# A hybrid decoder step on one core: depthwise taps on VectorE alone, PEER queries block by block, V rows 20 steps behind U rows

## The reference

```python
xn = rmsnorm(h, g_mix);  z = xn @ w_in                       # 1024 -> 512 pool, 512 val, 512 gate
ya = pool_mixer(z[:, :512])                                  # trailing means over 2/4/8/16, minus token, @ w_pool, * scale
u  = z[:, 512:1024] * sigmoid(z[:, 1024:])
yb = silu(layernorm(causal_depthwise_conv(u, w_dw, 31 taps) + b_dw))
h  = h + concat(ya, yb) @ w_out
x  = rmsnorm(h, g_ffn)
q  = (x @ w_q)                                               # 8 heads, 2 halves of 128 channels
s  = q @ sub_keys^T                                          # 128 scores for each half
sv, si = top_k(s, 16)                                        # for each half
cand = sv[half 0][:, None] + sv[half 1][None, :]             # 256 candidates
top_s, top_j = top_k(cand, 16); eidx = (si0 * 128 + si1)[top_j]
gate = softmax(top_s)
coef = gate * gelu(x . u_tab[eidx])                          # a row of 1024 numbers for each (token, head, k)
h  = h + sum(coef * v_tab[eidx])                             # again a row of 1024 numbers each
h  = h + (p @ w_ple_proj) * sigmoid(rmsnorm(h, g_ple) @ w_ple_gate)
y  = rmsnorm(h, g_final)
```

## Time and profile before

| | |
|---|---|
| median of 3 runs | 3163.8 us |
| the profiled execution, its time | 3164.09 us |
| its span, first to last instruction | 3162.3 us |
| mean granted TensorE clock | 0.965 |
| busy: TensorE matmul / VectorE / ScalarE / GpSimd | 2740.3 / 2224.3 / 836.8 / 2096.6 us |
| DMA: moved, mean rate over the span | 1165.84 MB, 369 GB/s |
| of it by the indirect gathers (queue 0) | 1107.43 MB |

### The profile page before, as it was taken

The page is one execution under the profiler, slowest core; times in us unless marked ns, Lnnn a source line. Parts: engine busy times, 40 slices in busy tenths (PEclk is TensorE's granted clock), DMA queues, the critical chain, the costliest instruction groups (busy, mean ns, idle before and its releaser), DMA issues.

```text
span 3162.3 us, 25895 instructions
## 1 busy us (share of the span) xinstructions
PE 2740.3 (87%) x7017; PEld 1261.3 (40%) x7017; DVE 2224.3 (70%) x5506; ACT 836.8 (26%) x2010; POOL 2096.6 (66%) x2238
## 2 busy tenths in 40 slices
PE   8978999899789988888888877799988898779878
PEld 7754444344334434443444432244333343223322
DVE  8946787988876666777777766666667777666553
ACT  2232323232222222222222222332222322222212
POOL 2533657667776677666766767777777777776773
PEclk9989999999999999999999999999999999999999
DMA  5216999999999999999999999999999999999995
GB/s 149 70 38 232 401 386 391 400 374 395 409 409 401 397 408 404 405 403 402 395 403 395 406 407 398 405 398 397 408 409 409 406 408 397 409 409 396 408 409 201
DMA packets 388084, 1165.84 MB, mean 369 GB/s; under 512 B 35769, under 2 KB 113161, under 8 KB 387941
## 3 DMA queue, kind: packets, MB, share of 16 engines
q0 software_dynamic: 304128, 1107.43, 88.8%
q1 hardware_dynamic: 83280, 55.92, 5.9%
q10 hardware_dynamic: 533, 0.83, 0.1%
HBM read 1158.88 MB, written 5.15 MB: 368 GB/s over the span
## 4 chain that ended last, share of the span: by engine, by line
DMA 29%; PE 23%; DVE 19%; POOL 15%; issue 7%; ACT 1%; DVEq 0%; ACTq 0%; POOLq 0%
DMA ex_u_row<-in_u_tab_dram,ex_eidx 22%; PE ex_acc L1547 14%; POOL ex_v_row L1007 8%; DVE ex_u_row L1654 7%; POOL ex_u_row L1007 7%; DMA ex_v_row<-in_v_tab_dram,ex_eidx 6%; PE ex_q L1286 4%; DMA ex_u_row<-in_u_tab_dram,ex_few_idx 1%; PE ex_q L1337 1%; DVE ex_same L1593 1%; DVE ex_same L1597 1%; DVE ex_idx L1600 1%; PE ex_s L1419 1%; DVE ex_top_at L1573 1%; DVE ex_top_at L1566 1%
## 5 line engine op out<-in xcount | busy, mean ns | idle before, releaser
L1547 PE MATMUL ex_acc<-ex_v_row,ex_diag 128*128 128x512 f32 (+1 forms) x4176 | 1982.6, 618 | 365.6 <-DMA ex_v_row<-in_v_tab_dram,ex_eidx 196.6
L1654 DVE CUSTOM_DVE_ANT_0 ex_u_row<-ex_u_row,ex_xn 128x1024 f32<-128x1024 f32 x1056 | 1270.2, 1217 | 750.5 <-DMA ex_u_row<-in_u_tab_dram,ex_eidx 713.5
L1547 PEld LDWEIGHTS ex_acc<-ex_v_row,ex_diag 128*128 128x128 f32 (+1 forms) x4176 | 775.1, 194 | 1481.1 <-issue 1183.3
L1007 POOL DMA_INDIRECT ex_v_row<-in_v_tab_dram,ex_eidx x1024 | 972.5, 950 | 487.3 <-issue 243.4
L1007 POOL DMA_INDIRECT ex_u_row<-in_u_tab_dram,ex_eidx x1024 | 976.4, 954 | 413.1 <-issue 266.1
L1113 ACT ACTIVATE ex_diag<-m_ident,ex_coef 128x128 f32<-128x128 f32 x1024 | 341.8, 392 | 546.1 <-PE ex_acc L1547 311.5
L1286 PE MATMUL ex_q<-m_mix,m_wq 128*128 128x384 f32 (+3 forms) x832 | 240.1, 443 | 1.9 <-PEq L86 1.9
L1202 ACT ACTIVATE ex_hact<-ex_hdot 128x16 f32<-128x16 f32 x66 | 14.2, 216 | 759.2 <-DVE ex_hdot L1654 759.1
L1286 PEld LDWEIGHTS ex_q<-m_mix,m_wq 128*128 128x128 f32 x832 | 143.7, 195 | 99.1 <-issue 62.7
L668 DVE SCALAR_TENSOR_TENSOR fr_mix<-fr_ufull,m_taps,fr_mix 128x256 f32<-128x256 f32 (+2 forms) x150 | 100.9, 673 | 4.9
L1050 ACT ACTIVATE ex_score<-ex_s,ex_rstd 128x128 f32<-128x128 f32 (+1 forms) x132 | 39.0, 363 | 231.8 <-PE ex_s L1297 118.4
(11 more groups left out here) (346 smaller groups left out, 1925.5 us busy)
## 6 DMA issues: line engine op xcount, KB each, us to landing
m_wq<-in_w_q_dram SPq DMA_DIRECT2D x32, 512.0 KB, 15.2
ex_u_row<-in_u_tab_dram,ex_eidx POOLq DMA_INDIRECT x1024, 11.0
ex_v_row<-in_v_tab_dram,ex_eidx POOLq DMA_INDIRECT x1024, 11.0
fr_w<-in_w_in_dram SPq DMA_DIRECT2D x12, 512.0 KB, 4.4
m_wq<-in_w_in_dram SPq DMA_DIRECT2D x12, 512.0 KB, 15.2
m_wq<-in_w_out_dram SPq DMA_DIRECT2D x8, 512.0 KB, 15.2
m_mix<-in_w_ple_gate_dram SPq DMA_DIRECT2D x8, 512.0 KB, 14.1
out_y_prompt_dram<-m_wq SPq DMA_DIRECT2D x7, 512.0 KB, 6.5
```

The lines of the kernel that those rows point to most:

```text
L1007: pool.indirect_dma_start(out=row[:, :], out_offset=None, in_=table, in_offset=bass.IndirectOffsetOnAxis(ap=picks(b)[:, k:k + 1], axis=0)) ...
L1547: last = nc.tensor.matmul(acc[0:rows(t), half, :], diag[:, tensor_sums(n) % DIAGS, 0:rows(t)], v_row[n % V_RING][:, half * HALF_D:(half + ...
L1654: nc.vector.tensor_tensor_reduce(out=u_row[n % U_RING][:, :], in0=u_row[n % U_RING][:, :], in1=xn[:, :], scale=1.0, scalar=0.0, op0=ALU.mu ...
```

## The change

1. `front`: taps go to two tiles in turn, even ones to `mix`, odd ones to `odd`, and each waits for the tap before the last (`Chain.but_one`); a `tensor_tensor` adds the two. VectorE does all 512 columns of the last channel group, `share_of_taps` is gone, and `add_part` is on VectorE. Five of the eight pool halves of the output projection are computed ahead of the layer norm, three between its steps.
2. Queries: the first two units are halves 0 and 1, then 2 and 3, of tile 0 (one unit each, two loads); then come halves 4 to 15 for four tiles, then halves 0 to 3 for tiles 1 to 3, whose weights are loaded a second time (56 loads of 512 KB instead of 52). Six units run before block 0 instead of twelve. `AHEAD` is 1, five score buffers replace two and a held one, picks come at steps 0 and 2 and the ranking at step 4 of a block, and none in block 0.
3. `pick` writes its indices directly (the casts go); in `rank_head` three pairs of operations over 256 elements become three over 512.
4. V rows are issued 20 steps behind U rows (`V_BEHIND`), and VectorE takes one to four V rows of each of blocks 1 to 29 (77 in all, added straight to the residual tile), and 8 and 10 of the two sample blocks. `ROW_LAG` puts such an add 21 steps behind its own dot.
5. The mixer for tiles 4 to 7 moves one to three blocks later, its products go to the `turn` banks instead of `q` and `s`, and from tap 93 on there are two taps per step. `xn` is made from the residual tile instead of from `turn`.
6. The embedding products of tile 7 and of the samples are made in block 61 instead of in the last two blocks.

```diff
+    def but_one(self, ins):
+        self.n += 1
+        ins.then_inc(self.sem, 1)
+        if self.n > 1:
+            self.eng.wait_ge(self.sem, self.n - 1)
...
-            share_of_taps()
-            for n in range(DC):
-                add_part(n)
...
-            pe.wait_ge(share_conved, TAPS)
...
+                even, odds, tap = mix[:, MC + c, lo:hi], odd[:, lo:hi], M.taps[:, c, :]
                 for k in range(TAPS):
+                    src, out = ufull[:, lo + k:hi + k], odds if k % 2 else even
...
+                        chain.but_one(nc.vector.scalar_tensor_tensor(out=out, in0=src, scalar=tap[:, k:k + 1], in1=out, op0=ALU.mult, op1=ALU.add))
+                chain.all()
+                ins = nc.vector.tensor_tensor(even, even, odds, ALU.add)
...
-AHEAD = 2
+AHEAD = 1
...
-EARLY = 12
+EARLY = 6
+SCORES = 5
+V_BEHIND = TOPK + 4
+ROW_LAG = V_BEHIND - TOPK + 1
...
+FIRST_TAP, PAIRED = 8 * TOPK + 6, 3 * TAPS
...
+def unit(s):
+    if s < ALONE:
+        return [(2 * s, 2 * s, 0, P), (2 * s + 1, 2 * s + 1, 0, P)], [(2 * s, 0), (2 * s + 1, 0)]
...
-VECTOR_KS = {PROMPT_BLOCKS: (2, 5, 8, 11, 14), PROMPT_BLOCKS + 1: (1, 3, 5, 7, 9, 11, 13)}
+VECTOR_KS = {b: (6, 10) if b < 9 else (6,) for b in range(1, 14)}
+VECTOR_KS.update({b: (3, 9) for b in range(14, 18)})
+VECTOR_KS.update({b: (1, 4, 7, 10) for b in range(18, 30)})
+VECTOR_KS.update({PROMPT_BLOCKS: (1, 3, 5, 7, 9, 11, 13, 14), PROMPT_BLOCKS + 1: (1, 2, 3, 5, 6, 7, 9, 10, 11, 13)})
...
-                    if b > 0:
-                        m = n - TOPK
+                    m = n - V_BEHIND
+                    if 0 <= m < BLOCKS * TOPK:
...
+                if b < PROMPT_BLOCKS:
+                    tokens = kept(blocks[b][0])
+                    dve.wait_ge(v_added, vector_sums(n))
+                    ins = nc.vector.scalar_tensor_tensor(out=tokens, in0=v_row[n % V_RING][:, :].rearrange("p (c e) -> p c e", c=DC),
+                                                         scalar=coef[b % 2][:, k:k + 1], in1=tokens, op0=ALU.mult, op1=ALU.add)
```

More of the change, by code:

```diff
@@ L119 @@
 W_RING = 4
+AHEAD_OF_NORM = 5
 WQ_RING = 3
-SHARED = SA - P
 def column(kind, i):
@@ L399, in _ @@
                 map_scaled(g)
-            for n in range(DC):
+            for n in range(AHEAD_OF_NORM):
                 part_kept(n)
@@ L1034, in query_out @@
             def query_out(s):
-                cols = sum(rows(t) for t in unit(s)[3])
+                cols = sum(rows(t) for _, t in unit(s)[1])
                 act.wait_ge(q_done, s + 1)
@@ L1273, in query @@
             def query(s):
-                load, _, at, tiles = unit(s)
-                cols = sum(rows(t) for t in tiles)
-                ready, count = loaded(load)
-                pe.wait_ge(ready, count)
                 if s >= 1:
@@ L1295, in scores @@
                     pe.wait_ge(score_out, s)
-                for j, t in enumerate(tiles):
+                for j, (half, t) in enumerate(unit(s)[1]):
                     last = nc.tensor.matmul(s_ps[0:rows(t), j * P:(j + 1) * P], qT[:, s % 2, j * P:j * P + rows(t)], keysT[:, half, :],
@@ L1573, in pick @@
                     last = nc.vector.max_index(at[:, 8:16], values[:, 8:16], left)
-                chain.step(last)
-                for j, t in enumerate(tiles):
-                    last = nc.vector.tensor_copy(si[0:rows(t), t, half, :], top_at[0:rows(t), j, :])
                 last.then_inc(picked, 1)
```

486 lines of the change are left out of this document (259 added, 227 removed), and 3 rows, old and new, of the table LATE_PRODUCT.

## The result

The changed kernel takes 3112.8 us, the median of 6 runs (3109.7 to 3113.9), beside 3163.9 for 6 runs of the kernel before; the ratio is 0.9838, interval 0.9826 to 0.9851. That is 51 us less, where 44 were forecast. The profiled execution took 3109.7 us, span 3107.9 against 3162.3: 54.4 us less. Both lie within the range, on the side that was forecast.

The account below looks back on a forecast made before the run. The DMA engines were taken to bound the middle, with little fetched in a front of some 300 us. Terms -45 + 2 - 5 + 2 + 6 - 4 = -44 gave 3119.5 us for the median, range 3096 to 3147.

Parts of the forecast that it names:

- Taps: First phase on VectorE: pitch 0.68 us for 512 columns and 0.42 for 256, ending 9.4 us earlier, at 145.6.
- pitch stays: Rival in the first phase: taps keep their 0.79 us pitch, VectorE ends 6.5 us later, kernel 3135 us; chance 0.10.
- First query: From the end of the taps to the first query: it starts 20 us earlier, at 195.5.
- Start of the blocks: Gathers run on from 224, 73.5 us earlier; less 11.5 for fewer rows issued and 17 for loads, -45 us.
- the load term: Weight loads left when gathers run on: 7 more than before at 2.4 us each, 17 us lost.
- V rows 20 behind and VectorE's rows: Middle blocks: V rows 20 steps behind gain 5 us (0 to 11); VectorE's adds cost 2 (0 to 24).
- Late mixer: Block 14 has 52 us of VectorE work against 43, blocks 8 and 13 have 46 and 45; +6 us (0 to 14).
- free lag: Late mixer: a ring of 8 less 4.3 steps in flight lets VectorE lag 3.7 steps, 9.5 us, without cost.
- First picks: Block 1: two picks and a ranking among four dots, some 22 us, just covered by gathers; +2 us (0 to 10).
- tile ends: Rival, each tile's second block: VectorE stops some 7 us for the last V row; 56 us, 3175; chance 0.05.
- GpSimd is held: Rival: VectorE's adds hold GpSimd's gathers, 24 us over 30 blocks and 4 in the tail, 3147 us; chance 0.12.
- Tail: Last U row to last V row: 6.4 us lost instead of 10.4, the chain behind unchanged; -4 us (-9 to +4).

Follow-up runs that it names:

- Runs 1 and 11: The changed kernel with each first-phase tap waiting for the tap just before it; ratios to the kernel before 1.0046 and 1.0056, on a slow chip.
- run 10: The changed kernel with each of the last 16 weight loads for queries made twice; 3139.9 us, ratio to the kernel before 0.9925.
- run 12: The kernel before with the two picks and the ranking of block 0 moved to before dot 15; ratio 1.0020, on a slow chip.
- run 2: The changed kernel with the whole first phase of the kernel before; ratio to the kernel before 1.0061, on a slow chip.
- run 9: The changed kernel with all prompt-block V rows on TensorE and V rows 16 steps behind; 3119.2 us beside 3162.0, ratio 0.9863.

## Why the prediction was right, point by point

- *Taps.* Forecast pitch 0.68 and 0.42, measured 0.66 and 0.40; end 145.6, measured 143.6. Runs 1 and 11 show that the wait makes it. The rival "pitch stays" is out. The rule of the Trainium skill ("VectorE: DVE Perf Modes", section "The DRAIN you can't avoid"), that the next operation waits for the empty pipe with or without a semaphore, does not hold for these adds: with a wait for the last but one they overlap by 0.08 us. The same section also says "A next op that is not held starts earlier", which the rival left out and which the trace agrees with.
- *First query.* Forecast 20 us earlier, measured 23.9. Of the 3.9 more, 2.0 are the taps; the rest are the products between them and the projection, which took 9.1 us where I had 10.8 (the variances 4.61 where I had 5). The 1.7 for the projection's first eight matmuls held: 1.89 instead of 3.59, as there is no stretch at the lower clock any more (granted 0.57 at 182 to 186 before, 1.00 from 143.6 to 191.5 now).
- *Start of the blocks.* Forecast -45. Measured at block 1: 60.4 corrected, less 5.0 for the bytes of the four loads more and less 2.3 for what five loads cost beyond their bytes (0.45 each, run 10; one load fewer is out at block 1): -53. The step held (gathers run on from 221, forecast 224); the load term was mis-sized, 7 x 2.4 = 17 where 7 x 1.73 = 12 was right, and the first query gave 4 more: -54, which agrees. Fewer units and the picks behind block 0 belong together (the kernel before, at run 12); the first phase is apart from them (run 2).
- *V rows 20 behind and VectorE's rows.* Forecast -5 and +2. Run 9 takes both out and loses 10.1 us by the traces. By block 5 the two parts have gained 10 (63.2 against 53.0), in blocks 1 to 5, where queries and V rows fill TensorE. I had written that work taken from TensorE is worth nothing in the middle, and named blocks 4 and 8 as exceptions, for 5 us; the exceptions were the term, and twice as large. From block 13 to 36 the two parts lose most of it again (9.9 to 1.8 apart) and from there to the end win it back (10.1); why, was not tried. Which of the two parts does it, run 9 does not tell.
- *Late mixer.* Forecast +6. Between blocks 13 and 20 the changed kernel loses 11.5. Three loads more fall into this stretch and cost 1.4 beyond their bytes (0.45 each), so 10.1 are left; run 9, with the same loads, loses 7.8, or 6.4. The block was seen rightly (52 us forecast, 50.5 measured), but I let it have 9.5 us of free lag, and it had less: block 14 alone cost 7.0, and run 9's block 15 6.6 though no V row stands on VectorE there. I had looked at the ring of U rows alone; what VectorE, when it is behind, also delays is the release of V rows, by its own adds (6.54 and 6.41) or by late coefficients (10.04 in run 9). What run 9 leaves out, VectorE's rows and the 4 steps more, makes the stretch longer by 3.7 us.
- *First picks, tile ends, port.* The 6.70 us behind the first picks are there and mostly covered: the corrected lead falls by 2.0 in block 1 (60.4 to 58.4), where I had 2. The tile end did not decide: VectorE stops 9.6 us at the second dot of block 49 (forecast some 7), and the block has 405 GB/s. "GpSimd is held" is out as a rival for the middle: block 29 with four adds has 404 GB/s. The holding itself is there: of 126 gathers that overlap one of the 77 adds 30 took over 1.5 us, and none of the other 834 of the first 30 blocks. Block 25 has 376 GB/s, with waits of GpSimd of 2.54 us for such an add and of 3.60 for a dot, so some of the 3.0 lost between blocks 20 and 36 may be theirs.
- *Tail.* Forecast 6.4 lost of 20 rows and -4 in all. The 20 rows lost 11.4, that is 1.0 more than before instead of 4 less: this step was wrong. The lead still grows, by 2.0 corrected, because of what I had taken as unchanged: from the last V row's issue to the end it is 37.0 us instead of 39.8. 1.7 of this is the last product, 13.92 us at a granted clock of 1.00 instead of 15.62 at 0.89, and 1.4 lies between the last V row's issue and VectorE's last sum (3081.65 and 3134.67), where before the embedding product of 3.60 us stood too. That the term's sign is right is luck. Run 10, with the same tail, needs 2.8 us more from the start of block 65 to its end, so these numbers are near what traces differ by.

So the time was right with terms wrong against each other: start -53.1 (forecast -45), blocks 1 to 13 -5.6 (+2 for the first picks and -5, so -3), blocks 13 to 20 +10.1 (+6), blocks 20 to 65 -3.8 (+2), tail -2.0 (-4). That makes -54.4 for the profiled execution, where the forecast was -44. The front, which makes nearly all of the gain, came out by its mechanism; that the middle and the tail came out near their sum is in part luck. The step that failed is the free lag of 9.5 us in the late mixer, with the tail's 6.4; the load price was too large (2.4 for 1.73) and the relief of TensorE in the first blocks too small (5 for 10).

Not tried: the changed kernel with VectorE's rows left in blocks 1 to 12 and from 20 on, and none between. By the ledger it could gain some 4 us, not the whole hole. Also not tried is the changed kernel with the late taps one per step to the end, which goes at the hole itself; and each of the two parts of run 9 alone on a chip like that of the result. No run takes out the merged lookups, the later place of the late mixer or the earlier embedding products by themselves.

## What to carry to other kernels

Where a resource is full in the middle, the time is made before it fills: here nearly the whole gain came from getting the first V row out 60 us earlier, 24 of them by a shorter first phase (run 2) and the rest, as far as the traces tell, by fewer units before block 0 together with no pick among the first dots. A buffer's release that hangs on a busy engine's order, directly or through a small result that another engine waits for, is not free because the engine has idle time on average: look at the block in which it has none. And when one such wait is taken out, look one block further before you say that it was the cause. Compare two kernels at block starts with the bytes that each has fetched by then, not by the clock alone and not by what it has issued.
